# A two-block transformer kernel: the turned activations kept with the two tiles' tokens interleaved

## What is computed

```python
h = rmsnorm(x, norm_g[i]);  mem_h = rmsnorm(mem, mem_norm_g[i])
proj = einsum('bsd,de->bse', h, w_in)        # 1024 x 11264 in layer 0, 1024 x 3584 in layer 1
o_mix = mixer(q, k, v of proj)               # banded attention in three dilations / grouped heads
kv = einsum('bnd,de->bne', mem_h, w_kv)      # 1024 x 1024
o_mem = softmax(q_mem k^T) v
x = x + concat(o_mix, o_mem) * silu(gate) @ w_out
```

## Time and profile before

| | before |
|---|---|
| median of 3 runs | 1149.97 us (1147.03 to 1153.93) |
| the profiled execution | 1149.28 us |
| its span, from the first to the last instruction | 1147.9 us |
| PE matmul busy | 1105.9 us (96%), 5515 matmuls |
| PE weight load busy | 917.1 us (80%), 5515 loads |
| DVE busy | 890.2 us (78%) |
| ACT busy | 746.9 us (65%) |
| DMA | 221.26 MB, 193 GB/s |

### The profile page before, as it was taken

One profiled execution on the slowest core, in us unless ns is written; L12 is line 12 of the kernel. 1 busy time (PEld: TensorE's weight loads), 2 busy tenths in 40 slices (PEclk: granted clock), 3 DMA queues, 4 the chain that ended last, 5 costly groups with the idle time before them and its releaser, 6 DMA issues.

```text
span 1147.9 us, 14686 instructions
## 1 busy us (share of the span) xinstructions
PE 1105.9 (96%) x5515; PEld 917.1 (80%) x5515; DVE 890.2 (78%) x1476; ACT 746.9 (65%) x1325; POOL 0.2 (0%) x4
## 2 busy tenths in 40 slices
PE   7999999999999999999999999999999999999996
PEld 5788888888787888888977787877778878787774
DVE  4756757777768867766578769999977886999996
ACT  5746665655666665577465557888855655688883
POOL 0000000000000000000000000000000000000000
PEclk9999999999999999999999899999999999999998
DMA  8654454443433455534452416999927332599991
GB/s 291 231 198 147 147 184 148 158 171 111 149 145 111 171 195 181 197 110 153 153 173 74 147 38 201 353 361 367 369 88 243 111 112 72 167 361 356 370 356 41
DMA packets 131844, 221.26 MB, mean 193 GB/s; under 512 B 6145, under 2 KB 77361, under 8 KB 131761
## 3 DMA queue, kind: packets, MB, share of 16 engines
q1 hardware_dynamic: 127920, 213.21, 54.4%
q10 hardware_dynamic: 3840, 6.98, 1.8%
HBM read 219.13 MB, written 1.05 MB: 192 GB/s over the span
## 4 chain that ended last, share of the span: by engine, by line
PE 78%; DVE 11%; ACT 6%; issue 2%; DMA 2%; ACTq 0%; DVEq 0%
PE bank L488 21%; PE bank L490 20%; PE bank L489 20%; PE bank L851 4%; PE bank L787 3%; DVE wL L441 2%; PE bank L637 1%; ACT wH L433 1%; DMA ring<-in_w_mem_kv 1%; PE bank L836 1%; PE bank L2274 1%; PE bank L2323 1%; ACT S L810 1%; PE bank L1735 1%; PE bank L2288 1%
## 5 line engine op out<-in xcount | busy, mean ns | idle before, releaser
L441 DVE TENSOR_TENSOR wL<-ring,wH 128x1024 fp32r<-128x1024 f32 (+1 forms) x316 | 375.3, 1212 | 127.4 <-ACT wH L433 126.2
L433 ACT ACTIVATE wH<-ring 128x1024 fp32r<-128x1024 f32 (+1 forms) x316 | 320.3, 1047 | 31.5 <-PE bank L490 14.1
L488 PE MATMUL bank<-wH,hTH 128*128 128x512 f32 (+2 forms) x592 | 235.7, 398 | 3.3 <-DVE wL L441 2.3
L490 PE MATMUL bank<-wH,hTL 128*128 128x512 f32 (+2 forms) x592 | 229.8, 388 | 0.0
L489 PE MATMUL bank<-wL,hTH 128*128 128x512 f32 (+2 forms) x592 | 229.3, 387 | 0.0
L488 PEld LDWEIGHTS bank<-wH,hTH 128*128 128x128 f32 x592 | 111.7, 189 | 25.9 <-DVE wL L441 4.5
L490 PEld LDWEIGHTS bank<-wH,hTL 128*128 128x128 f32 x592 | 111.5, 188 | 21.9
L489 PEld LDWEIGHTS bank<-wL,hTH 128*128 128x128 f32 x592 | 111.8, 189 | 20.2 <-issue 0.5
L488 PE MATMUL bank<-wH,xgH 128*128 128x512 f32 x256 | 104.5, 408 | 0.0
L490 PE MATMUL bank<-wH,xgL 128*128 128x512 f32 x256 | 100.4, 392 | 0.0
L489 PE MATMUL bank<-wL,xgH 128*128 128x512 f32 x256 | 100.0, 391 | 0.0
(11 more groups left out here) (296 smaller groups left out, 1866.2 us busy)
## 6 DMA issues: line engine op xcount, KB each, us to landing
ring<-in_w_in_a SPq DMA_DIRECT2D x44, 1024.0 KB, 5.1
ring<-in_w_out SPq DMA_DIRECT2D x20, 1024.0 KB, 4.9
ring<-in_w_down SPq DMA_DIRECT2D x20, 1024.0 KB, 7.2
ring<-in_w_gate SPq DMA_DIRECT2D x36, 512.0 KB, 5.4
ring<-in_w_up SPq DMA_DIRECT2D x36, 512.0 KB, 7.1
ring<-in_w_in_b SPq DMA_DIRECT2D x14, 1024.0 KB, 5.2
ring<-in_w_mem_kv SPq DMA_DIRECT2D x8, 1024.0 KB, 7.1
ring<-in_w_in SPq DMA_DIRECT2D x8, 1024.0 KB, 5.4
```

The lines of the kernel that those rows point to most:

```text
L433: act.e.activation(quarter_parts(q)[0], quarter_in_ring(q), COPY).then_inc(w_high, 1)
L441: dve.e.tensor_tensor(lo, quarter_in_ring(q), hi.bitcast(F32), SUB).then_inc(w_low, 1)
L488: pe.e.matmul(o, a[0], b[0], start=first, stop=False)
L490: return pe.e.matmul(o, a[1], b[0], start=False, stop=last)
```

## The change

`hT` and `mhT` keep their size and place, but token `n` of tile `i` now lies at `2n + i` instead of `128i + n`. A view (`by_turns`) gives the buffers the indices chunk, tile, token, with a step of two elements (8 bytes) from token to token. What PE loads is the same 128 values in the same order, read at every second element. What ACT and DVE write is the same: a chunk of 256 tokens is written as two runs of 128, each with a step of 8 bytes; where one tile is written alone, every second element is written. What they read from PSUM stays contiguous; DVE's read of the high part has the step of 8 bytes too. No instruction is added, removed or moved, and no wait changes. Number formats and products stay.

```diff
-    hT = [sb(f"hT{n}", P, 8, TOK, dt=F32R) for n in "HL"]
+    def by_turns(z):
+        return z[:, :, :].rearrange("p k (n i) -> p k i n", i=2)
+
+    hT = [by_turns(sb(f"hT{n}", P, 8, TOK, dt=F32R)) for n in "HL"]
...
-    mhT = [sb("mhTH", P, 8, TOK, at=("G", 0), dt=F32R), sb("mhTL", P, 8, TOK, at=("arena", 0), dt=F32R)]
+    mhT = [by_turns(sb("mhTH", P, 8, TOK, at=("G", 0), dt=F32R)), by_turns(sb("mhTL", P, 8, TOK, at=("arena", 0), dt=F32R))]
...
-                    mm = mm3(b.t[:, 0:width], [z[:, kk, i * P:(i + 1) * P] for z in lhs], [z[:, k, :] for z in w], kk == 0, kk == 7)
+                    mm = mm3(b.t[:, 0:width], [z[:, kk, i, :] for z in lhs], [z[:, k, :] for z in w], kk == 0, kk == 7)
...
+        def by_tiles(o):
+            return o.rearrange("p j (i n) -> p j i n", i=2)
...
-                        act.e.activation(dst[:, j0 + j, :], o[:, j, :], COPY, scale=gain[:, j0 + j:j0 + j + 1]).then_inc(*act.did("high", *key, j0))
+                        act.e.activation(dst[:, j0 + j, :, :], by_tiles(o)[:, j, :, :], COPY, scale=gain[:, j0 + j:j0 + j + 1]).then_inc(*act.did("high", *key, j0))
...
-                        dve.e.scalar_tensor_tensor(dst[1][:, j0 + j, :], o[:, j, :], gain[:, j0 + j:j0 + j + 1],
-                                                   dst[0][:, j0 + j, :].bitcast(F32), MUL, SUB).then_inc(*dve.did(*key, j0))
+                        dve.e.scalar_tensor_tensor(dst[1][:, j0 + j, :, :], by_tiles(o)[:, j, :, :], gain[:, j0 + j:j0 + j + 1],
+                                                   dst[0][:, j0 + j, :, :].bitcast(F32), MUL, SUB).then_inc(*dve.did(*key, j0))
...
-                act.e.activation(hT[0][:, j0:j0 + 4, i * P:(i + 1) * P], bank_of["xT", name, i, j0].t[:, :].rearrange("p (j n) -> p j n", j=4),
+                act.e.activation(hT[0][:, j0:j0 + 4, i, :], bank_of["xT", name, i, j0].t[:, :].rearrange("p (j n) -> p j n", j=4),
                                  COPY).then_inc(*act.did("high", "xT", name, i, j0))
...
-                dve.e.tensor_tensor(hT[1][:, j0:j0 + 4, i * P:(i + 1) * P], bank_of["xT", name, i, j0].t[:, :].rearrange("p (j n) -> p j n", j=4),
-                                    hT[0][:, j0:j0 + 4, i * P:(i + 1) * P].bitcast(F32), SUB).then_inc(*dve.did("xT", name, i, j0))
+                dve.e.tensor_tensor(hT[1][:, j0:j0 + 4, i, :], bank_of["xT", name, i, j0].t[:, :].rearrange("p (j n) -> p j n", j=4),
+                                    hT[0][:, j0:j0 + 4, i, :].bitcast(F32), SUB).then_inc(*dve.did("xT", name, i, j0))
```

More of the change, by code:

```diff
@@ L544, in pe_proj_by_tiles @@
                     pe.wait_ge((w_low, q + kk // 2 + 1), ready(kk, i))
-                    mm = mm3(b.t[:, 0:width], [z[:, kk, i * P:(i + 1) * P] for z in lhs], [z[:, kk % 2, :] for z in w], kk == 0, kk == 7)
+                    mm = mm3(b.t[:, 0:width], [z[:, kk, i, :] for z in lhs], [z[:, kk % 2, :] for z in w], kk == 0, kk == 7)
                     if i == 1 and kk % 2 == 1:
@@ L653, in act_flip_high @@
                 if gain is None:
-                    act.e.activation(dst[:, j0:j0 + 2, :], o, COPY).then_inc(*act.did("high", *key, j0))
+                    act.e.activation(dst[:, j0:j0 + 2, :, :], by_tiles(o), COPY).then_inc(*act.did("high", *key, j0))
                 else:
                     for j in range(2):
-                        act.e.activation(dst[:, j0 + j, :], o[:, j, :], COPY, scale=gain[:, j0 + j:j0 + j + 1]).then_inc(*act.did("high", *key, j0))
+                        act.e.activation(dst[:, j0 + j, :, :], by_tiles(o)[:, j, :, :], COPY, scale=gain[:, j0 + j:j0 + j + 1]).then_inc(*act.did("high", *key, j0))
         def dve_flip_low(key, n, dst, gain=None, meanwhile=nothing):
@@ L664, in dve_flip_low @@
                 if gain is None:
-                    dve.e.tensor_tensor(dst[1][:, j0:j0 + 2, :], o, dst[0][:, j0:j0 + 2, :].bitcast(F32), SUB).then_inc(*dve.did(*key, j0))
+                    dve.e.tensor_tensor(dst[1][:, j0:j0 + 2, :, :], by_tiles(o), dst[0][:, j0:j0 + 2, :, :].bitcast(F32), SUB).then_inc(*dve.did(*key, j0))
                 else:
                     for j in range(2):
-                        dve.e.scalar_tensor_tensor(dst[1][:, j0 + j, :], o[:, j, :], gain[:, j0 + j:j0 + j + 1],
-                                                   dst[0][:, j0 + j, :].bitcast(F32), MUL, SUB).then_inc(*dve.did(*key, j0))
+                        dve.e.scalar_tensor_tensor(dst[1][:, j0 + j, :, :], by_tiles(o)[:, j, :, :], gain[:, j0 + j:j0 + j + 1],
+                                                   dst[0][:, j0 + j, :, :].bitcast(F32), MUL, SUB).then_inc(*dve.did(*key, j0))
         def act_root(key, ss, n, scale, eps):
@@ L1647, in act_flip_exit @@
                 act.wait_ge(at("turned", "xT", "exit", 0, j0))
-                act.e.activation(hT[0][:, j0:j0 + 4, 0:P], bank_of["xT", "exit", 0, j0].t[:, :].rearrange("p (j n) -> p j n", j=4),
+                act.e.activation(hT[0][:, j0:j0 + 4, 0, :], bank_of["xT", "exit", 0, j0].t[:, :].rearrange("p (j n) -> p j n", j=4),
                                  COPY).then_inc(*act.did("high", "exit", way, j0))
@@ L1653, in dve_flip_exit @@
                 dve.wait_ge(at("high", "exit", way, j0))
-                dve.e.tensor_tensor(hT[1][:, j0:j0 + 4, 0:P], bank_of["xT", "exit", 0, j0].t[:, :].rearrange("p (j n) -> p j n", j=4),
-                                    hT[0][:, j0:j0 + 4, 0:P].bitcast(F32), SUB).then_inc(first_turned, 1)
+                dve.e.tensor_tensor(hT[1][:, j0:j0 + 4, 0, :], bank_of["xT", "exit", 0, j0].t[:, :].rearrange("p (j n) -> p j n", j=4),
+                                    hT[0][:, j0:j0 + 4, 0, :].bitcast(F32), SUB).then_inc(first_turned, 1)
         def dve_rotate(src, dst, n, w, c, s, *name, scratch=T0):
@@ L2130, in pe_all @@
                                 mm = mm3(b.t[:, f_ * TOK:(f_ + 1) * TOK], [z[:, k_, n * 256 + f_ * P:n * 256 + f_ * P + P] for z in w],
-                                         [z[:, 2 * q + k_, :] for z in hT], q + k_ + f_ == 0, 2 * q + k_ == 7 and f_ == 1)
+                                         [z[:, 2 * q + k_, :, :] for z in hT], q + k_ + f_ == 0, 2 * q + k_ == 7 and f_ == 1)
                         if n == 0 and q == 3:
```

## The result

| | before | after |
|---|---|---|
| median of 9 runs | 1149.97 us (1147.03 to 1154.16) | 1157.53 us (1155.04 to 1161.1) |
| ratio to before, with its 95% interval | | 1.0068, 1.0044 to 1.0092 |
| the profiled execution | 1149.28 us | 1157.45 us |
| its span | 1147.9 us | 1156.1 us |
| mean granted clock | 0.989 | 0.989 |

I had forecast 1139.5 us. The page of the profile of after, its parts 1 and 4 and four groups of part 5, answers to the earlier trace rows; lines 488, 489 and 490 are now 491, 492 and 493.

The account below looks back on a forecast made before the run. PE was taken to bound the kernel, through matmuls on hT and mhT. 1149.3 - 12.4 (loads) + 2.5 (writes) = 1139.4, given as 1139.5 us; 1125 to 1145 if right, 1125 to 1160 overall.

Parts of the forecast that it names:

- What bounds the kernel: Whole kernel: PE holds 78% of the chain; each 512-column matmul costs 227 ns, 13 ns more than its columns.
- How many count: Matmuls on hT and mhT that set the end: 1255 from 40 to 560 us plus 290 in the second block.
- rival C: Every matmul on hT: stepped loads fetch twice as much, excess doubles, +13 ns each, 1174 to 1180 us; chance 0.13.
- The price of a load: Loads of hT and mhT with the 8-byte step: -8 ns per matmul, bounds -13 to +13 ns.
- the 1545 matmuls of my sum: Matmuls on hT and mhT counted as setting the end, at 8 ns each a gain of 12.4 us.
- The row on which I leaned: Constant matmuls that stream one repeated zero: 219 ns against 227 for real data, the source of -8 ns.
- The two neighbours that I had: 416 columns at half clock, 346 ns against 347; full float32 with 512 columns, 430 ns against 427.
- rival A: Loads of hT and mhT: the step changes nothing on PE, writes cheap, about 1151 us; chance 0.20.
- The writes: ACT's and DVE's writes of hT and mhT: 1 ns per element more, 0 to 10.8 us in all, 2.5 us taken.
- The cover that I named: First block's second layer: PE has up to four quarters of 2.7 us in advance; without it up to 7.2 us added.
- B: Loads unchanged, but ACT's and DVE's writes dear and PE's cover gone: 3.6 to 10.8 us more, about 1156 us; chance 0.11.
- D: Loads of hT and mhT become the limit at 265 ns each, 71 us added, 1220 us; chance 0.03.

Follow-up runs that it names:

- run 3: Kernel before, but in the first block PE loads hT and mhT with a step of 8 bytes from densely written rows; ratio 1.0036, median 1154.45 us.
- run 5: Kernel before with the whole change, writes and loads by turns, in the first block alone; ratio 1.0056, median 1154.92 us.
- Run 7: Kernel before, but the first block's hT and mhT are loaded with a step of 32 bytes across four chunks; ratio 1.0243, median 1177.31 us.
- run 1: Stand-alone groups of 48 matmuls with varied load and stream steps, other engines idle; at 512 columns 227 ns dense, 233 with a step of 8 bytes.
- run 6: Stand-alone groups of 48 matmuls, dense against 8-byte-step loads at eleven widths from 320 to 512 columns; at 512 columns 227.1 against 233.3 ns.

## Why the prediction was wrong

**What bounds the kernel: right.** PE's matmuls on `hT` and `mhT` set the end, and a price of some nanoseconds on each comes out in the total.

**How many count: right at this price.** The first block has 1392 matmuls of 512 columns on `hT` and 192 on `mhT`, of which I put 1255 on the chain, 79%. With the measured price that gives 1584 x (233.3 - 227.7) = 8.9 us, x 0.79 = 7.0 us. The traces show 6.3, 7.0 and 7.3 us (after, runs 3 and 5; the latter two had a half-clock stretch in the place of before's, which puts after at 7.0 too). With the dearer load it is 1584 x 16.9 = 26.8 us against 26.7 measured: nearly all of them count then, as rival C said of dearer loads, and the 79% would have fallen 6 us short. Run 7's wait for four chunks lies in the 26.7 too; it can't be large, since the distances behind matmuls on `hT` and `mhT` have grown by 25.8 us in all. In the second block I counted 290, but half of its 384 have 416 or 452 columns and pay nothing. The other half gives 192 x 0.75 x 5.6 ns = 0.8 us, which is what after loses there against run 3, and 7.0 + 0.8 = 7.8 us stands against the 8.2 of the spans. The 0.4 us between them is within what half-clock stretches in other places can do.

**The price of a load: this step failed, in its sign.** I took -8 ns from the distance between data and one repeated value, and the guess that a stepped load, taking each 8-byte word once, would meet the stream less often. It is +6.6 ns once the pace has settled and +5.6 on average: with the 1545 matmuls of my sum, 1545 x 5.6 = 8.7 us more instead of 12.4 less. The row on which I leaned differs in the stream and not in the load. It could show that the excess is shared with the stream's reading, and this holds (run 1), but not which load has less of it. The two neighbours that I had, the excess gone at half clock and in full float32, spoke of the stream as well. I gave a guess without a single row on a load the largest chance; the bounds, -13 to +13, held the value. Why the step costs 6.6 ns at 512 columns and nothing at 508 isn't shown; what is shown is that the step of the loads, by itself, costs it.

**The average is below the settled price** because in before, too, not every distance is 227: 17% of those on `hT` in the first block are 229 to 245 ns, 40% of the distances in steps that stand behind an attention's products or transposes (lines 787 and 836) and 10% in the others, and with the step the mean of all is the settled 233.3. This was to be seen before the run. I wrote under rival A that the excess is the same whatever buffer is loaded; in before the ten matmuls on `yT2`, with dense loads and at granted clock 1.00, have 231 ns ((658.11 - 656.03) / 9):

```profile
656.03 0.40 PE L490 MATMUL bank<-wH,yT2L 128*128 128x512 f32 x1
...
658.11 0.40 PE L490 MATMUL bank<-wH,yT2L 128*128 128x512 f32 x1
```

**The writes: the price was too high, and so was the sum.** I took 1 ns per element from steps on 8 values; DVE's writes cost nothing, ACT's 7 to 13 ns for 256 elements and 31 for 512. The cover that I named hid what there was: 2.5 us forecast, 0.5 at the end of the first block. The Trainium skill ("Vector Engine (DVE) Microarchitecture Reference", section 5.2), by which writes that hop every element run below the full rate, isn't borne out at this step: 475 ns after against 476 before.

**The rivals.** A and B fall with the pace of 233; that B's 1156 us lies near the measured 1157.5 is chance, since its dear writes didn't come. C had the right sign and place; its price was twice the real one and its mechanism, twice the fetches and twice the excess, fails on the widths (run 6). D doesn't come in: the load by itself is 118 ns at this step and 173 at 12 bytes. The Trainium skill's "SBUF — State Buffer" (Specifications), by which the full rate needs two hits in a line, agrees with the loads' own pace to 7% (117.9 against 110.6 ns; 173 at 12 bytes, which has fewer than two) and not with the matmuls' at 512 columns. Its row also gives each cross to a new line a penalty, and a step of 8 bytes crosses twice as many; I had left that out when I took it to stand for rival A. The rest of my list held: no `xg`, `gh` or `yTH` load changed, and the experts' stretch kept its length: from 707 to 840 us the traces of before, after and run 3 keep their distances from one another to 0.1 us.

**What stays open.** Why 512 columns with a dense load in its place settle at 544 cycles while every other step, and every start 1 to 16 words off, had a mean of 550 to 587, and why the step's price appears between 508 and 512 columns. The settled paces seen most often, 448, 544 and 560 cycles, are multiples of 16, as if load and stream fell into a common beat. Run 6 was to test that over its widths and speaks against it as a rule: 464, 480 and 496 columns with dense loads have 504, 521 and 536 cycles, none of them a multiple of 16. No layout or place tried had a lower pace than the kernel before, so there is no version here that beats it.

## What to carry over

Where a matmul on real data shows an excess over its columns, measure the candidates alone before touching a layout: groups of 48 matmuls in one short program gave each price to 1 ns, and with the count of such matmuls on the chain it gave the kernel's change to 1 us (a dearer load came out 6 us above the same count). Read the granted clock of every group before comparing two: three of run 6's were at half clock, and their numbers look like a property of the step. Keep what PE loads dense and aligned, and test at the width that the kernel uses, since 508 and 512 columns gave different verdicts. When a row differs from the case in two operands, say which of the two it can speak for before taking a number from it.

## What the runs showed of the hardware

- A load with a step of 8 bytes costs by the width streamed: +6.2 to 6.6 ns at 512 columns, 0 within 2 ns at nine of the ten next narrower widths tried, and 5.7 ns less at 488.
- Where a dense load or stream starts matters as much as a step of 8 bytes: 229 to 237 ns from 1 to 16 words off the kernel's places, 227 on them.
- With 128 columns streamed, at granted clock 1.00, matmuls follow each other at 110.6 ns with dense loads, 117.9 with a step of 8 bytes and 173 with one of 12. At granted clock 0.50 it is 213 ns with 12 bytes, 233 with 16, 240 with 32 and 222 with 64.
- A stream with a step of 8 bytes takes twice the time (453 ns from start to start, where dense has 227), at steps of the load of 1 and 2 alike.
- DVE writes and reads runs with a step of 8 bytes at the pace of dense ones: 128x256 in 475 ns (476 dense), 128x512 in 684 (682). ACT's writes take 503 to 509 ns for 128x256 (496) and 624 for 128x512 (593).
- Busy ACT and DVE don't change the pace of the matmuls by 1 ns.
